# Two attentions of a two-block kernel: the first one's outputs scaled by ScalarE with remainders made a tile later, and the forgetting attention's outputs kept with two heads on the partitions

## The chip, the cores and the metric

One core of a Trainium2 chip runs the whole program once. The metric is the device time of that execution in microseconds. Engines are named as the profile names them: PE (TensorE), PEld (its weight loads), DVE (VectorE), ACT (ScalarE), POOL (GpSimd), SP (the engine whose queue issues DMAs).

## What is computed

Two transformer blocks over 1024 tokens of width 1024. The first has a convolution, a differential attention and a mixture of experts; the second mixes four branches, one of them a forgetting attention. The change concerns the two causal attentions:

```
def diff_attention(q, k, v, lam, ...):            # 4 heads, each with 2 score sets of 64, values of 128
    s = einsum("bqhcd,bkhcd->bhcqk", qi, k) * scale
    p = softmax(where(mask, s, -inf))
    a = p[:, :, 0] - lam * p[:, :, 1]
    o = einsum("bhqk,bkhe->bqhe", a, v)           # then rms_norm over each head's 128

def _fox(z, b_f):                                 # 4 heads of 64
    c = cumsum(log_sigmoid(f_pre + b_f), axis=1)
    s = einsum('bqhd,bkhd->bhqk', qi, k) + cqi[..., :, None] - c_keys[:, :, None, :]
    s = where(kpos <= qpos, s, -inf)
    out = einsum('bhqk,bkhd->bqhd', softmax(s), v)
```

## The kernel before

Both attentions are one function, `soft_attention`, called with the tag `da` (paired: `outs` = 1 output per pair, `dv` = 128, four pairs, one for each head) and with the tag `fx` (not paired: two heads per pair, `outs` = 2, `dv` = 64, two pairs). It works through units `u` = (pair `i`, query tile `t` of 128 queries), eight tiles a pair, each against `t + 1` key tiles, for two score sets `x` = 0, 1. Queries and keys are kept as a rounded part (made by ACT, L838, L841 and for fx L843) and a remainder (made by DVE, L880 for keys, L885 for queries, each 64x1024), so that scores are sums over both. Those of the next pair are made during this one: ACT rounds at the end of the units t = 1 to 4 and DVE makes the remainders at the end of the same units.

Each engine has its own queue, written out by hand and run in order:

- PE, per unit u: `scores(u + 1, 1)` (L789 to L791; waits for exps of unit u, x = 1, since the bank is the same), `scores(u + 2, 0)` (waits for exps of u + 1, x = 0), `turn_weights(u)` (L804: transposes of the exps, in chunks of up to four tiles that go alternately to two banks; a chunk waits until the one two before it was copied out), `weigh(u - 1)` (L816: the turned weights times the values; waits for the finish of unit u - 3, whose bank it takes).
- DVE, per unit u: `combine(u)` (L906 reciprocal of the row sums into `share`; in da also L909 and L911, which join both exps), `finish(u - 2)` (L918: the output bank times `share`, into `o`; waits for weigh), `peaks(u + 1, 1)` and `peaks(u + 2, 0)` (L901: row maxima of the scores), `keep_turned(u)` (L895: in fx alone, copies of the turned exps of x = 1), then the remainders.
- ACT, per unit u: `exps(u + 1, 0)`, `exps(u + 1, 1)` (L850; each waits for its peaks and reads out the row sum), `keep_turned(u)` (L860: copies of turned exps, of x = 0), then the rounding.

In da the output of a unit has queries on the partitions, 128 columns; it is normalised by the stage `on`. In fx a unit's output also has queries on the partitions, 64 columns for each of two heads, in columns 256 to 511 of `o_soft`; the window attention puts its own into columns 0 to 255. After the window attention and the mLSTM, the stage `tm` (`turn`: L1706 copies a token tile on DVE, L1716 transposes it in pieces of 128, L1726 copies out on ACT) turns all 512 columns into `yT[:, 4:8]`. The mLSTM's output goes to `o_mlstm`. The turned weights of fx lie in `yT[:, 4:8]` while the attention runs. PSUM has eight banks: 0 to 3 scores, 4 and 5 turned chunks, 6 and 7 outputs of alternate units.

Elsewhere, in `rwkv_chunks` (earlier in the second block), L2796 is a matmul whose stationary operand is 64 columns wide and whose output lies on the partitions 0 to 63 and 64 to 127 in turn, with 128 columns:

```
def sum_own(t):
    for j in range(2):
        for n, left in enumerate((vt, uw[:, :, 0:N])):
            for e in range(2):
                last = mm(pair(5, P)[side(e), j], left[:, 2 * j + e, :], n12[:, 1 - n, 2 * j + e, :],
                          start=(n == 0), stop=(n == 1))
```

## Time and profile before

| | |
|---|---|
| median of 3 runs | 3487.06 us (3474.16 to 3507.37) |
| the profiled execution | 3475.44 us, span 3473.8 us |
| PE busy | 2908.6 us (84%) |
| DVE busy | 1807.6 us (52%) |
| ACT busy | 1340.1 us (39%) |
| mean granted clock of TensorE | 0.90 of full |
| da (first attention) | 376 to about 532 us |
| fx (forgetting attention) | 2262 to about 2372 us |
| tm (turning of `o_soft`) | 2546 to about 2555 us |

Busy times are for the whole span; the stages follow each other with a barrier of all engines between them, so an engine's share of the whole says nothing about one stage. The clock column of a window is the granted clock of TensorE as a share of its full 2.4 GHz; 0.5 is its lower level, 1.2 GHz. One matmul of fp32 operands is two instructions, each with its weight load.

### The profile page before, as it was taken

The numbers are of one execution on the slowest core, as the hardware profiler recorded it, in microseconds if no ns is written. First come the engines' busy times: TensorE is split into PE (matmuls) and PEld (weight loads), VectorE is DVE, ScalarE is ACT, GpSimd is POOL, SyncE is SP. The second block draws the span as 40 slices with busy tenths as digits, with TensorE's granted clock in tenths as the row PEclk, the third lists the DMA queues.
The fourth block names the chain that finished last, engine by engine and source line by source line (L and its number), as shares of the span: only waits on it lengthen the run. The fifth ranks groups of instructions, "written<-read, shape, count | busy, mean of one in ns | idle before, by whom it ended". The sixth has DMA issues, their size and how long they took to land. (4 is left out here: it accounts for less than half of the span.)

```text
span 3473.8 us, 42813 instructions
## 1 busy us (share of the span) xinstructions
PE 2908.6 (84%) x14243; PEld 2349.4 (68%) x14243; DVE 1807.6 (52%) x2199; ACT 1340.1 (39%) x1942; POOL 287.0 (8%) x215
## 2 busy tenths in 40 slices
PE   3996587998938999997399979278777899999998
PEld 2784575665736888886377778166656688887876
DVE  2896773111437999996435255654434433333334
ACT  3222562111316888885323124254434322222232
POOL 0221000000011111111122110000200000000000
PEclk8998788999968999998599989578769799999999
DMA  2115102110249999996412220201203111111122
GB/s 80 37 49 186 44 1 79 42 48 12 85 129 332 412 412 412 412 412 265 158 43 73 65 70 2 108 2 25 49 21 130 49 48 48 48 48 33 48 100 79
DMA packets 247386, 408.19 MB, mean 118 GB/s; under 512 B 39453, under 2 KB 157268, under 8 KB 247284
## 3 DMA queue, kind: packets, MB, share of 16 engines
q1 hardware_dynamic: 215428, 343.54, 27.7%
q10 hardware_dynamic: 22464, 33.32, 2.7%
q0 software_dynamic: 9392, 29.99, 2.6%
q8 instruction: 62, 1.02, 0.1%
q14 instruction: 40, 0.33, 0.0%
HBM read 342.72 MB, written 64.07 MB: 117 GB/s over the span
## 5 line engine op out<-in xcount | busy, mean ns | idle before, releaser
L1610 DVE TENSOR_TENSOR e_w_lo<-e_ring,e_w_hi 128x1024 fp32r<-128x1024 f32 x384 | 446.5, 1217 | 48.7 <-ACT e_w_hi L1537 48.7
L1537 ACT CAST e_w_hi<-e_ring 128x1024 fp32r<-128x1024 f32 x384 | 377.6, 1049 | 38.0 <-PE banks L1467 27.4
L1939 PE MATMUL banks<-h_hi,u_w_hi 128*128 128x512 f32 x704 | 274.8, 390 | 10.5 <-DVE u_w_lo L1973 10.5
L1940 PE MATMUL banks<-h_lo,u_w_hi 128*128 128x512 f32 x704 | 274.7, 390 | 0.0
L1941 PE MATMUL banks<-h_hi,u_w_lo 128*128 128x512 f32 x704 | 274.5, 390 | 0.0
L1465 PE MATMUL banks<-e_w_hi,e_xT_hi 128*128 128x512 f32 x512 | 203.1, 397 | 0.0
L1467 PE MATMUL banks<-e_w_hi,e_xT_lo 128*128 128x512 f32 x512 | 200.1, 391 | 0.0
L1466 PE MATMUL banks<-e_w_lo,e_xT_hi 128*128 128x512 f32 x512 | 199.9, 390 | 0.0
L522 DVE SCALAR_TENSOR_TENSOR conv<-x_first,vectors,conv 128x1024 f32<-128x1024 f32 x120 | 183.8, 1531 | 9.0
L1939 PEld LDWEIGHTS banks<-h_hi,u_w_hi 128*128 128x128 f32 x704 | 132.6, 188 | 38.4 <-issue 10.9
L1941 PEld LDWEIGHTS banks<-h_hi,u_w_lo 128*128 128x128 f32 x704 | 132.6, 188 | 27.8
L1940 PEld LDWEIGHTS banks<-h_lo,u_w_hi 128*128 128x128 f32 x704 | 132.6, 188 | 27.4
L1793 PE MATMUL banks<-fd_w_hi,fd_s_hi 128*128 128x512 f32 x352 | 138.4, 393 | 10.2 <-DVE fd_s_lo L1852 9.0
L381 PE MATMUL banks<-h_hi,z_w_hi 128*128 128x512 f32 x320 | 129.1, 403 | 16.6 <-POOL z_w_lo L473 16.6
L1795 PE MATMUL banks<-fd_w_hi,fd_s_lo 128*128 128x512 f32 x352 | 137.5, 391 | 0.0
L1794 PE MATMUL banks<-fd_w_lo,fd_s_hi 128*128 128x512 f32 x352 | 137.5, 391 | 0.0
L330 PE MATMUL banks<-consts,n_xn 128*128 128x128 f32 x192 | 44.7, 414 | 98.7 <-ACT n_xn L279 98.6
L383 PE MATMUL banks<-h_hi,z_w_lo 128*128 128x512 f32 x320 | 127.2, 398 | 0.0
L382 PE MATMUL banks<-h_lo,z_w_hi 128*128 128x512 f32 x320 | 127.2, 397 | 0.0
L1978 DVE TENSOR_SCALAR yT<-yT,vectors 128x1024 f32<-128x1024 f32 x22 | 17.9, 814 | 194.2 <-ACT yT L1953 194.2
L1948 ACT ACTIVATE u_w_hi<-yT 128x1024 fp32r<-128x1024 f32 x44 | 46.5, 1057 | 178.9 <-PE banks L1941 172.7
L1973 DVE TENSOR_TENSOR u_w_lo<-yT,u_w_hi 128x1024 fp32r<-128x1024 f32 x44 | 53.8, 1222 | 115.2 <-ACT u_w_hi L1948 115.2
(528 smaller groups left out, 6689.8 us busy)
## 6 DMA issues: line engine op xcount, KB each, us to landing
e_ring<-in_w_gate_e_dram SPq DMA_DIRECT2D x128, 512.0 KB, 8.0
e_ring<-in_w_up_e_dram SPq DMA_DIRECT2D x128, 512.0 KB, 9.6
e_ring<-in_w_down_e_dram SPq DMA_DIRECT2D x128, 512.0 KB, 7.2
yT<-in_ffn_w_up_dram SPq DMA_DIRECT2D x44, 512.0 KB, 3.9
expert_results<-nothing SPq DMA_DIRECT2D x1, 16384.0 KB, 55.5
expert_results<-e_y ACTq DMA_DIRECT2D x32, 512.0 KB, 7.8
fd_w<-in_ffn_w_down_dram SPq DMA_DIRECT2D x44, 256.0 KB, 2.6
z_w<-in_w_in_dram SPq DMA_DIRECT2D x19, 512.0 KB, 3.9
```

The costliest lines, as they stand in the source:

```text
L522: nc.vector.scalar_tensor_tensor(conv[:, c, :], y[:, c, j:j + S], tap(j), conv[:, c, :], ALU.mult, ALU.add)
L1465: mm(bank, xT_hi[:, b, k, :], w_hi[:, part, cols], start=(k == 0), stop=False)
L1466: mm(bank, xT_hi[:, b, k, :], w_lo[:, part, cols], start=False, stop=False)
L1467: last = mm(bank, xT_lo[:, b, k, :], w_hi[:, part, cols], start=False, stop=(k == KT - 1))
L1537: nc.scalar.copy(w_hi[:, part, :], experts.ring[:, slot, :]).then_inc(w_rounded, 1)
L1610: tt(w_lo[:, part, :], experts.ring[:, slot, :], w_hi[:, part, :].bitcast(F32), ALU.subtract).then_inc(w_split, 1)
L1793: nc.tensor.matmul(K.ps[:, t, :], s_hi[:, b, tokens], w_hi[:, b, :], start=first, stop=False)
L1794: nc.tensor.matmul(K.ps[:, t, :], s_hi[:, b, tokens], w_lo[:, b, :], start=False, stop=False)
L1795: mm = nc.tensor.matmul(K.ps[:, t, :], s_lo[:, b, tokens], w_hi[:, b, :], start=False, stop=last)
L1939: nc.tensor.matmul(bank, w_hi[:, up, k, :], h_hi[:, k, tokens], start=(k == 0), stop=False)
L1940: nc.tensor.matmul(bank, w_hi[:, up, k, :], h_lo[:, k, tokens], start=False, stop=False)
L1941: mm = nc.tensor.matmul(bank, w_lo[:, up, k, :], h_hi[:, k, tokens], start=False, stop=(k == KT - 1))
```

## The change

Three edits. In da, DVE's `finish` is replaced by one on ACT (a copy with a per-partition scale), placed between `exps(u + 1, 0)` and `exps(u + 1, 1)`, for unit u - 2. In both attentions DVE makes the remainders one unit later (t = 2 to 5); ACT rounds where it did. In fx `weigh` exchanges its operands: a head's 64 value columns are stationary, the turned weights move, and the two heads' outputs lie on the partitions 0 to 63 and 64 to 127 with queries along the columns. Two more matmuls per unit spread `share` over the same layout, into the other columns of the same bank; DVE copies that, drains, and multiplies, straight into `yT[:, 6:8]`. So `o_soft` has half its columns, `tm` turns half as much, and the turned weights of odd units lie in `o_mlstm`. A new semaphore `shared` tells that `share` is there.

```diff
--- before.py
+++ after.py
@@ -705,7 +705,8 @@
-def soft_attention(K, tag, q_tiles, k_tiles, values, v_col, dv, o, o_col, paired, exps_room, turned_room, decay=None):
+def soft_attention(K, tag, q_tiles, k_tiles, values, v_col, dv, o, paired, exps_room, turned_room, decay=None):
@@ -724,6 +725,7 @@
     kept = [K.sem(f"{tag}_kept{x}") for x in range(outs)]
     k_made, q_made, k_split, q_split, filled, scored, peaked, exped, combined, turned, weighed, finished = (K.sem(f"{tag}_{n}") for n in
         ("k_made", "q_made", "k_split", "q_split", "filled", "scored", "peaked", "exped", "combined", "turned", "weighed", "finished"))
+    shared = K.sem(f"{tag}_shared")
     decay_landed = [K.sem(f"{tag}_decay_landed{i}") for i in range(pairs)] if decay is not None else None
     with ExitStack() as scope, nc.Block() as block:
         q1 = K.sb(scope, f"{tag}_q1", [P, 4, S], F32R)
@@ -745,7 +747,10 @@
             return K.ps[:, 2 * x:2 * x + 2, :].rearrange("p b n -> p (b n)")[:, 0:n]
         def out_bank(u):
-            return K.ps[:, 6 + u % 2, 0:outs * dv]
+            return K.ps[:, 6 + u % 2, 0:P]
+        def share_bank(u):
+            return K.ps[:, 6 + u % 2, P:2 * P]
         def exps_of(u, x):
             return exps_room[u % 2][x][:, 0:units[u][1] + 1, :]
@@ -811,10 +816,18 @@
                     pe.wait_ge(finished, u - 1)
                 for x in range(outs):
                     pe.wait_ge(kept[x], last_chunk[u, x][1])
-                    col = v_col + (i if paired else 2 * i + x) * dv
+                if paired:
                     for j in range(t + 1):
-                        last = mm(out_bank(u)[:, x * dv:(x + 1) * dv], turned_room[u % 2][x][:, j, :], values[:, j, col:col + dv],
+                        last = mm(out_bank(u), turned_room[u % 2][0][:, j, :], values[:, j, v_col + i * dv:v_col + (i + 1) * dv],
                                   start=(j == 0), stop=(j == t))
+                else:
+                    pe.wait_ge(shared, u + 1)
+                    for j in range(t + 1):
+                        for x in range(2):
+                            col = v_col + (2 * i + x) * dv
+                            mm(out_bank(u)[own(x)], values[:, j, col:col + dv], turned_room[u % 2][x][:, j, :], start=(j == 0), stop=(j == t))
+                    for x in range(2):
+                        last = mm(share_bank(u)[own(x)], share[:, x, t:t + 1].to_broadcast([P, HD]), K.const("ident"), start=True, stop=True)
                 last.then_inc(weighed, 1)
             for u, x in ((0, 0), (0, 1), (1, 0)):
@@ -860,6 +873,12 @@
                     nc.scalar.activation(turned_room[u % 2][x][:, j0:j0 + count, :],
                                          K.ps[:, 4 + c % 2, 0:count * P].rearrange("p (j n) -> p j n", n=P), ACT.Copy).then_inc(kept[x], 1)
+            def finish(u):
+                i, t = units[u]
+                act.wait_ge(shared, u + 1)
+                act.wait_ge(weighed, u + 1)
+                nc.scalar.activation(o[:, t, i * dv:(i + 1) * dv], out_bank(u), ACT.Copy, scale=share[:, 0, t:t + 1]).then_inc(finished, 1)
             for x in range(2):
                 round_keys(0, x)
                 round_queries(0, x)
@@ -869,9 +888,14 @@
                 if u + 1 < len(units):
                     for x in range(2):
                         exps(u + 1, x)
+                        if paired and u >= 2 and not x:
+                            finish(u - 2)
                 keep_turned(u)
                 if 1 <= t <= 4 and i + 1 < pairs:
                     (round_keys if t % 2 else round_queries)(i + 1, (t - 1) // 2)
+            if paired:
+                for u in (len(units) - 3, len(units) - 2, len(units) - 1):
+                    finish(u)
         @block.vector
         def _(dve):
@@ -903,7 +927,7 @@
             def combine(u):
                 i, t = units[u]
                 dve.wait_ge(exped, 2 * u + 2)
-                nc.vector.reciprocal(share[:, :, t], mass[:, :, t])
+                nc.vector.reciprocal(share[:, :, t], mass[:, :, t]).then_inc(shared, 1)
                 dve.drain()
                 if paired:
                     nc.vector.tensor_scalar(factor[:, t:t + 1], mass[:, 0, t:t + 1], share[:, 1, t:t + 1], K.lam[:], ALU.mult, ALU.mult)
@@ -914,9 +938,10 @@
             def finish(u):
                 i, t = units[u]
                 dve.wait_ge(weighed, u + 1)
-                place = o[:, t, o_col + i * outs * dv:o_col + (i + 1) * outs * dv]
-                nc.vector.tensor_tensor(place.rearrange("p (x n) -> p x n", x=outs), out_bank(u).rearrange("p (x n) -> p x n", x=outs),
-                                        share[:, 0:outs, t].unsqueeze(2).to_broadcast([P, outs, dv]), ALU.mult).then_inc(finished, 1)
+                place = o[:, i, t * P:(t + 1) * P]
+                nc.vector.tensor_copy(place, share_bank(u))
+                dve.drain()
+                nc.vector.tensor_tensor(place, out_bank(u), place, ALU.mult).then_inc(finished, 1)
             def fill(dst, value):
                 ones = K.const("ones")[0:HD, 0:1].to_broadcast([HD, S])
@@ -935,17 +960,18 @@
                 peaks(u, x)
             for u, (i, t) in enumerate(units):
                 combine(u)
-                if u >= 2:
+                if not paired and u >= 2:
                     finish(u - 2)
                 if u + 1 < len(units):
                     peaks(u + 1, 1)
                 if u + 2 < len(units):
                     peaks(u + 2, 0)
                 keep_turned(u)
-                if 1 <= t <= 4 and i + 1 < pairs:
-                    (split_keys if t % 2 else split_queries)(i + 1, (t - 1) // 2)
-            for u in (len(units) - 2, len(units) - 1):
-                finish(u)
+                if 2 <= t <= 5 and i + 1 < pairs:
+                    (split_queries if t % 2 else split_keys)(i + 1, (t - 2) // 2)
+            if not paired:
+                for u in (len(units) - 2, len(units) - 1):
+                    finish(u)
             dve.drain()
@@ -2988,7 +3014,7 @@
             with ExitStack() as exps_scope:
                 exps = K.sb(exps_scope, "da_exps", [P, 2, NT, P])
                 room = lambda n: qkv[:, :, HALF + n * P:HALF + (n + 1) * P]
-                soft_attention(K, "da", qkT[:, 0:HEADS], qkT[:, HEADS:2 * HEADS], qkv, 2 * HALF, VD, o, 0, True,
+                soft_attention(K, "da", qkT[:, 0:HEADS], qkT[:, HEADS:2 * HEADS], qkv, 2 * HALF, VD, o, True,
                                [[exps[:, b], room(2 + b)] for b in range(2)], [[room(b)] for b in range(2)])
             conv = K.sb(right, "conv_again", [P, CT, S], side="right")
             oT = K.sb(right, "oT", [P, HEADS, S], side="right")
@@ -3059,7 +3085,7 @@
         K.window_bias, K.sinks = (K.sb(scope, name, shape, side="right")
                                   for name, shape in (("window_bias", [P, 4, 2 * P]), ("sinks", [P, 4])))
         K.mlstm_keys = K.sb(scope, "mlstm_keys", [P, 4 * NT], side="right")
-        o = K.sb(scope, "o_soft", [P, NT, 2 * RW], side="right")
+        o = K.sb(scope, "o_soft", [P, NT, RW], side="right")
         o_mlstm = K.sb(scope, "o_mlstm", [P, NT, RW], side="right")
         Z["values"], Z["mlstm_o"] = sb("values", [P, NT, 3 * RW]), sb("mlstm_o_kept", [P, 2, S])
         values = Z["values"]
@@ -3074,11 +3100,12 @@
                              (Z["total"][:, 0, :], mlstm["rise"][:, 0], mlstm["rise"][:, 1])])
             tiles_of = lambda ap: ap.rearrange("p (j n) -> p j n", n=P)
             exps = [[tiles_of(gates[:, 0, :]), tiles_of(gates[:, 1, :])], [tiles_of(gates[:, 2, :]), tiles_of(Z["mlstm"][:, 0, 0:S])]]
-            turned = [[tiles_of(yT[:, 4 + 2 * b + n, :]) for n in range(2)] for b in range(2)]
-            soft_attention(K, "fx", Z["fox_q"][:], Z["fox_k"], values, RW, HD, o, RW, False, exps, turned, decay=decay)
+            flat = o_mlstm[:].rearrange("p t n -> p (t n)")
+            turned = [[tiles_of(yT[:, 4 + n, :]) for n in range(2)], [tiles_of(flat[:, n * S:(n + 1) * S]) for n in range(2)]]
+            soft_attention(K, "fx", Z["fox_q"][:], Z["fox_k"], values, RW, HD, yT[:, 6:8, :], False, exps, turned, decay=decay)
         window_attention(K, "sw", R["swa_q"], R["swa_k"], values, 2 * RW, o, 0)
         mlstm_attention(K, "ml", mlstm, values, 0, o_mlstm, 0)
-        turn(K, "tm", o, yT[:, 4:8, :])
+        turn(K, "tm", o, yT[:, 4:6, :])
         group_norm_and_turn(K, "mn", o_mlstm[:], 4, K.vec("mlstm_norm_2", 0, 2), yT[:, 2:4, :], gate=Z["mlstm_o"][:])
     K.recycle()
     return yT
```

## Rows read from the trace of the kernel before

**Rows 1.** Windows of da and fx: us, busy (x instructions) by engine, clock, DMA, GB/s
```profile
376.00:533.00 157.00, 116.39 (x688) 102.10 (x688) 114.95 (x213) 96.65 (x203) 0.00 (x0) 0.86 0.00 1
2262.00:2374.00 112.00, 86.43 (x560) 80.31 (x560) 58.73 (x105) 53.23 (x105) 2.11 (x4) 0.80 0.01 1
```

**Rows 2.** Waits: who <- for whom: us in total, times, longest; da, then fx
```profile
ACT qkv L850 <- DVE da_low L901: 50.9, 32, 3.0
...
DVE da_q L885 <- ACT da_q L841: 9.0, 6, 1.8
...
DVE da_k L880 <- ACT da_k L838: 8.5, 6, 1.7
...
DVE fx_k L880 <- ACT fx_k L838: 1.2, 2, 0.6
```

**Rows 3.** Timeline of da, third pair: start, us, engine, line, op [idle <-releaser]
```profile
468.72 2.13 ACT L838 ACTIVATE da_k<-x_first 64x1024 fp32r<-64x1024 f32 x2
...
469.80 1.22 DVE L880 TENSOR_TENSOR da_k<-x_first,da_k 64x1024 fp32r<-64x1024 f32 x1 [1.24 <-ACT da_k L838]
470.87 0.69 ACT L850 ACTIVATE da_exps<-banks,da_low 128x512 f32<-128x512 f32 x1
...
471.70 0.79 PE L789 MATMUL banks<-da_k,da_q 128*128 128x512 f32 x1 [2.30 <-ACT da_exps L850]
...
472.97 0.69 ACT L850 ACTIVATE qkv<-banks,da_low 128x512 f32<-128x512 f32 x1 [1.32 <-DVE da_low L901]
...
474.15 0.49 ACT L860 ACTIVATE qkv<-banks 128x384 f32<-128x384 f32 x1 [0.40 <-PE banks L804]
...
479.17 0.79 ACT L850 ACTIVATE qkv<-banks,da_low 128x640 f32<-128x640 f32 x1 [2.82 <-DVE da_low L901]
...
492.34 1.01 ACT L850 ACTIVATE qkv<-banks,da_low 128x896 f32<-128x896 f32 x1 [3.01 <-DVE da_low L901]
...
493.47 0.17 DVE L906 RECIPROCAL da_share<-da_mass 128x2 f32<-128x2 f32 x1
```

**Rows 4.** The finishing line L918: forms with ns minimum/median/maximum
```profile
L918 DVE TENSOR_TENSOR qkv<-banks,da_share x32: 281/283/293, 395.8 to 531.4; 128x128 f32<-128x128 f32 x32
```

**Rows 5.** Timeline of fx, one tile of the second pair (t = 5)
```profile
2343.40 0.48 PE L789 MATMUL banks<-fx_k,fx_q 128*128 128x512 f32 x1
...
2343.63 0.29 DVE L918 TENSOR_TENSOR o_soft<-banks,fx_share 128x128 f32<-128x128 f32 x1 [0.88 <-PE banks L816]
...
2344.56 2.26 DVE L901 TENSOR_REDUCE fx_low<-banks 128x1 f32<-128x896 f32 x2 [0.64 <-PE banks L791]
...
2345.68 1.01 ACT L850 ACTIVATE z_gates<-banks,fx_low 128x896 f32<-128x896 f32 x1 [3.56 <-DVE fx_low L901]
...
2347.41 0.84 PE L804 MATMUL banks<-consts,z_mlstm 128*128 128x128 f32 x6 [1.20 <-ACT yT L860]
...
2348.10 2.34 PE L816 MATMUL banks<-values,yT 128*128 128x64 f32 x20
...
2350.25 0.48 PE L789 MATMUL banks<-fx_k,fx_q 128*128 128x512 f32 x1
```

**Rows 6.** Timeline of fx, the weighing of the next tile, at the lower clock
```profile
2355.48 5.22 PE L816 MATMUL banks<-values,yT 128*128 128x64 f32 x24
```

**Rows 7.** Timeline of PE where L2796 stands between forms of other shape
```profile
2153.99 0.58 PE L2814 MATMUL banks<-rs_q,rs_diagonal 128*128 128x32 f32 x4
2154.51 0.44 PE L2796 MATMUL banks<-rs_n,rs_vt 128*64 128x128 f32 x4
2154.78 0.39 PE L2796 MATMUL banks<-rs_n,rs_uw 128*64 128x128 f32 x4
...
2155.21 0.39 PE L2796 MATMUL banks<-rs_n,rs_uw 128*64 128x128 f32 x4
2155.53 0.44 PE L2743 MATMUL banks<-consts,z_rwkv 128*128 128x128 f32 x2
```

**Rows 8.** Groups by line in tm: count, busy us, mean ns, idle before
```profile
L1716 PE MATMUL banks<-consts,tm_stage 128*128 128x128 f32 x32 | 6.9, 383 | 2.8 <-DVE tm_stage L1706 2.2 <-issue 0.4
```

## The prediction

> **What bounds the kernel now.** The page comes first: it shows a program of many stages one after the other, each between barriers, so an edit is worth what it changes in its own stage. The busy shares of whole engines say nothing here. The stretches come next [rows 1]. The first attention (tag da) lasts 157 us with PE, DVE and ACT each busy 97 to 116 us; the forgetting attention (tag fx) lasts 112 us with PE busy 86 and DVE and ACT under 60. So da is bound by a ring of three engines, fx mostly by PE and what stands in series with it. The third stage touched, tm (the turning of `o`), lasts about 9 us. Together they are 278 us, 8% of the 3473.8 us span, so 1% of the kernel (35 us) would be an eighth of them.
>
> Then the waits of these stretches [rows 2]. In da ACT waits 50.9 us in 32 times for DVE's peaks (L901), always before the second exps; DVE itself waits 9.0 and 8.5 us at L885 and L880, the remainders, for ACT's rounded copies (6 times each: three changes of head pair, four splits each). In fx that wait is 1.2 us.
>
> Last the timelines. In da [rows 3] the tile t=1 of the last but one pair: ACT rounds keys from 468.72, DVE stands 1.24 us before L880 and splits until 471.02, and only then comes combine, although the second exps it needs were done before ACT took up the rounding at 468.72. The second exps of the next tile so start at 472.97 after 1.32 us of waiting, the one after at 479.17 after 2.82. In fx [rows 5] one tile's turn of the ring is 6.85 us (2343.40 to 2350.25), everything in series: scores on PE, peaks from 2344.56, exps from 2345.68, ACT's turned copy, PE's second turning from 2347.41, and then weigh(u-1), 20 instructions from 2348.10 to 2350.25, ahead of the next scores. The turned chunks share two banks, so the second head's turning waits for ACT's copy, which stands behind exps(u+1, 1). Weigh is thus paid in full there.
>
> **da, finish moved to ACT.** DVE loses 32 L918 of 0.283 us [rows 4], of which about 0.21 from start to next start is paid where DVE is full. ACT gains one scaled copy of 128x128 per tile; that operation is not in the stage. Bounds: nothing, to the 0.79 us of a 128x640 exps [rows 3]; nearest in kind is its own DVE form, so 0.3 us. It lies between exps(u+1, 0) and exps(u+1, 1), where ACT waits 1.6 us on average [rows 2], so it is hidden; if that cover were gone, 28 x 0.3 = 8 us. Queued behind its wait for weigh(u-2) is exps(u+1, 1), for which combine waits; weigh(u-2) ends before the scores those exps need, as both stand in PE's order, so it adds nothing.
>
> **da, remainders a tile later.** I follow the two queues through the change of pair of rows 3, every instruction with the length it has there before. Tile 2: combine(2) starts at 468.7 instead of 471.0, and exps(3, 1) come right after exps(3, 0) at 471.7 instead of 472.97. But the turned copy of tile 2 stays at 474.15: PE takes scores(4, 0) first, at 471.70, which wait for exps(3, 0) of 470.87, and those stand behind ACT's rounding. So of the first wait nothing is kept. Tile 3: the keys' remainder, its input long there, fills DVE from 474.3 to 475.5, combine(3) ends at 476.7, peaks(4, 1) at 477.4, and exps(4, 1) start there instead of at 479.17: 1.7 us. The turned copy, which now waits for PE, comes 1.6 earlier and with it ACT's next rounding. Tile 4: the same again, exps(5, 0) 1.6 and exps(5, 1), after the finish on ACT, 3.1 us earlier, the turned copy, again bound by PE, 2.4. Tile 5: combine(5) and peaks(6, 1) back to back end at 488.2, where exps(6, 1) start instead of at 492.34: 4.1. Then the fourth remainder, which now stands in a tile where DVE is full, costs 1.2 back: combine(6) starts at 490.6 instead of 493.47, and peaks(7, 1), with finish gone, come 3.1 earlier. From tile 7 to tile 1 of the next pair PE is the bound and passes the 3.1 on. Three changes: 9.3 us. The last pair has no remainders to make and gains five times 0.21: 1.0. Together 10.3. The ends: nothing (ACT and PE set the pace everywhere as in tile 2), and all 17.5 us of waits plus 28 x 0.21 = 23 us; I take the middle because the hand-followed queues show both kinds of tile.
>
> **fx, weigh with two heads on the partitions.** Stationary is now a head's 64 columns of values, moving the 128 columns of turned weights; 288 instructions (2 passes x 72 key tiles x 2 heads) stay 288, since only the roles of the operands change. Before: 20 in 2.34 us and, next to it, 2.15 from start to start, 0.11 each; at the lower clock level 24 in 5.22, 0.21 each [rows 5, 6]. The same form already stands in the kernel, L2796 (128*64, output 128x128, sides alternating): two groups of four take from 2154.78 to 2155.21, 0.054 an instruction [rows 7]; at half the clock I take twice that. About 68 of the 288 ran at the lower level (both groups of 24 and the first small ones), so 220 x 0.057 + 68 x 0.10 = 19.4 us. Added are the shares: two matmuls per unit, 64 instructions, at 0.054 with a quarter slower: 4.2 us. A stationary operand repeated from one column is not in the rows; from below it costs nothing, from above the 0.11 of a full one, 7 us; I take the middle form's.
>
> The change of array shape twice a unit: L2814 to L2796 0.52 us for four, first L2796 group 0.27 instead of 0.215, L2796 to L2743 0.32 instead of 0.215 [rows 7]: about 0.2 us a unit, 3.2 us over 16. If every switch waited for a matmul to run out (a group of four takes 0.39, less three spacings of 0.054: 0.23), 32 of them would be 7.4 us, 4.2 more. The Trainium skill, TensorEngine Tiling (Array Packing), section Tiling Modes, says that changing the mode, unlike changing the tile, drains TensorE; the row shows a switch but less than such a full run-out, and the sum goes by the row. Net 19.4 - 4.2 - 3.2 = 12.0; at t=1 to 3 of the first pair ACT's rounding is the bound and hides part: 11.5 kept.
>
> **fx, finish on DVE** becomes copy, drain, multiply: 0.28 + 0.08 + 0.29 against 0.29 [rows 4], 0.37 more. In the large tiles it is covered: L918 starts at 2343.63, peaks only at 2344.56 [rows 5]. In about 7 small tiles peaks follow at once, and at the very end it is bare: +2.9 us. Uncovered everywhere: 16 x 0.37 = 6. The wait for `shared` is long met when weigh comes.
>
> **fx, remainders.** One change of pair; waits of 1.2 [rows 2]. The split at t=1 leaves a tight tile and that at t=5 falls into DVE's wait for weigh: -2 us (0 to -4).
>
> **tm** turns two tiles of 128 instead of four: 16 of 32 L1716 go, 0.2 us each from start to start at the lower clock (PE busy 6.9 us for 32 [rows 8]): 3.4 less, of which 3.0 in the ring with DVE's and ACT's copies (1 to 4). The smaller `o` and the new place of the turned weights move no work.
>
> **Sum**: -10.3 - 11.5 + 2.9 - 2.0 - 3.0 = -23.9 us. The profiled execution took 3475.4 (its span and 1.6 around it): 3451.5. It lies 11.6 under the median 3487.06 of three runs that spread over 33 us; against the median the forecast is 3463.
>
> **Rivals.** (1) Little is kept: in da the ACT-PE chain of the first step holds at all four splits, and in fx the next wait takes half of weigh's gain. For it: exps(3, 0) behind rounding; against it: ACT waits 50.9 us for DVE. -1 - 5.8 + 2.9 - 1 - 2 = -7: 3480. (2) All waits and the whole of weigh are kept: -23 - 12 - 4 - 4 + 0.4 = -43: 3444. For it: the series ring of rows 5; against it: splits still cost their 1.2 us. (3) Slower: TensorE's clock. In fx it was granted 0.80 on average [rows 1], and the group of 24 after PE's idle time ran at the 1.2 GHz level [rows 6]. Weigh is the dense part; halved, PE is idle for a larger share. New PE work is about 86 - 12 = 74 us at 0.80; the gain is eaten when it stretches by a third, at a mean clock of 0.61; at 0.50 it stretches by 0.6, +44: 3507. Against it: the ring gets shorter in time too, and its idle parts (peaks, exps) don't grow. The Trainium skill, TensorE: Matmul & The Clock Gate, section "A second HAM failure mode", says that frequent small idle times between groups of matmuls make the clock swing between its levels; the fx rows agree in kind. (4) Full run-out at each switch: 3467.
>
> **Chances.** Forecast 0.56, (1) 0.20, (2) 0.12, (3) 0.06, (4) 0.06. The forecast's own range is 3452 to 3473. Reaching into (1) and (2), and leaving their far ends and (3) out, 3441 to 3485. 1% is about what a measurement of this kernel can tell from no change; 3452 is the bound: below it lie (2) and an edge of the forecast, 0.17; slower by 1% (3522) needs (3) in da too: 0.03; between them 0.80.
>
> **What would show it.** In the profile after: weigh at 0.054 an instruction, and fx about 100 us; L880 and L885 of da with no wait for ACT, da about 147 us; ACT's scaled copy 0.3 us, with no wait for PE before it; tm about 6 us. It is wrong if the new finish on ACT waits for PE, if fx's granted clock is under 0.7, or if other stages differ by more than these.

## The result and the profile after

Eight runs of the changed kernel had a median of 3465.06 us (3462.80 to 3473.57), eight of the kernel before 3492.11 (3474.16 to 3507.37). The ratio is 0.9926, with a 95% interval of 0.9904 to 0.9949: 27 us of medians against the 24 forecast, less than 1%. The profiled execution took 3470.72 us, only 4.7 under that of before and 19 over the 3451.5 that the prediction gave for it, a gap to be explained below.

The stretches first (us, then busy time and instructions of PE, its weight loads, DVE, ACT and POOL, granted clock, DMA share, GB/s), as in [rows 1]. da is 7.5 us shorter by these windows, fx 13 us; DVE has given 6.7 us away in da and ACT has taken 9.5; in fx PE has given 14.5 us away, and its clock has risen from 0.80 to 0.86.

```profile
372.50:522.00 149.50, 111.13 (x688) 98.61 (x688) 108.23 (x182) 106.14 (x235) 0.00 (x0) 0.89 0.00 1
2272.00:2371.00 99.00, 71.98 (x624) 60.51 (x624) 61.94 (x121) 52.74 (x105) 2.11 (x4) 0.86 0.01 1
```

The windows have some slack at their edges. Below a stage is measured from the start of its first reciprocal (L906 before, L930 after) to the end of its last finish (L918; after, L880 in da and L944 in fx):

```profile
L930 DVE RECIPROCAL da_share<-da_mass x32: 150/167/169, 383.8 to 513.5; 128x2 f32<-128x2 f32 x32
...
L880 ACT ACTIVATE qkv<-banks,da_share x32: 351/368/388, 391.8 to 520.0; 128x128 f32<-128x128 f32 x32
...
L930 DVE RECIPROCAL fx_share<-fx_mass x16: 153/158/169, 2285.4 to 2360.3; 128x2 f32<-128x2 f32 x16
...
L944 DVE TENSOR_TENSOR yT<-banks,yT x16: 290/292/293, 2291.4 to 2369.2; 128x128 f32<-128x128 f32 x16
```

So da is 520.4 - 383.8 = 136.6 us (144.4 before, whose first reciprocal stood at 387.3 and whose last finish [rows 4] at 531.4) and fx 84.1 us (96.7 before). tm went from 8.8 to 6.0 us; 16 turnings are left, as against [rows 8] (ns minimum/median/maximum, first and last start):

```profile
L1742 PE MATMUL banks<-consts,tm_stage x16: 418/421/474, 2546.2 to 2550.9; 128*128 128x128 f32 x16
```

Together -7.8 - 12.6 - 2.8 = -23.2 us, against -23.9 forecast. The windows give 149.5 us for da and 99.0 for fx, where the prediction had about 147 and 100.

**da, the waits** after (engine line waited for: us, times, longest), to be set beside [rows 2]:

```profile
ACT qkv L863 <- DVE da_low L925: 24.3, 26, 2.4
...
DVE da_low L925 <- PE banks L796: 22.8, 22, 2.8
...
ACT qkv L873 <- PE banks L809: 9.9, 8, 1.8
...
ACT qkv L880 <- PE banks L821: 5.7, 8, 1.4
...
DVE da_share L930 <- ACT qkv L863: 5.1, 7, 1.3
```

ACT's wait for the peaks has gone from 50.9 to 24.3 us, and the two rows of DVE waiting for ACT's rounded copies are gone. In their place DVE waits for the scores and ACT for the turnings, both from PE: the bound has moved to PE with ACT. The new finish (L880) waits for PE in 8 of 32 tiles, which the forecast had excluded.

**da, the change of pair of [rows 3]** in the timeline after (start, us, engine, line, operation, idle before it):

```profile
465.77 1.21 DVE L904 TENSOR_TENSOR da_k<-x_first,da_k 64x1024 fp32r<-64x1024 f32 x1
...
469.02 0.80 ACT L863 ACTIVATE qkv<-banks,da_low 128x640 f32<-128x640 f32 x1 [0.87 <-DVE da_low L925]
...
469.99 1.22 DVE L909 TENSOR_TENSOR da_q<-x_first,da_q 64x1024 fp32r<-64x1024 f32 x1
...
472.57 0.90 ACT L863 ACTIVATE da_exps<-banks,da_low 128x768 f32<-128x768 f32 x1
...
473.47 0.36 ACT L880 ACTIVATE qkv<-banks,da_share 128x128 f32<-128x128 f32 x1
473.72 0.90 ACT L863 ACTIVATE qkv<-banks,da_low 128x768 f32<-128x768 f32 x1
...
480.22 1.01 ACT L863 ACTIVATE qkv<-banks,da_low 128x896 f32<-128x896 f32 x1 [0.96 <-DVE da_low L925]
...
481.60 1.22 DVE L909 TENSOR_TENSOR da_q<-x_first,da_q 64x1024 fp32r<-64x1024 f32 x1
...
482.85 0.17 DVE L930 RECIPROCAL da_share<-da_mass 128x2 f32<-128x2 f32 x1
```

The splits (L904, L909) start with no wait, and the fourth (481.60) stands bare in front of the reciprocal of tile 6. At the start of this stretch the kernel after is already 8.15 us ahead (reciprocal of tile 1: 457.41 against 465.56). With that taken off, the steps followed come out like this, in us earlier than before:

| | forecast | measured |
|---|---|---|
| turned copy, tile 2 | 0 | 0.3 |
| exps(4, 1) | 1.7 | 2.0 |
| exps(5, 1) | 3.1 | 3.6 |
| turned copy, tile 4 | 2.4 | 2.2 |
| exps(6, 1) | 4.1 | 4.0 |
| combine(6) | 2.9 | 2.5 |
| exps(7, 1) | 3.1 | 2.65 |

**fx, the tile of [rows 5] and the one behind it**, after:

```profile
2347.53 0.50 PE L794 MATMUL banks<-fx_k,fx_q 128*128 128x512 f32 x1
...
2348.01 0.29 DVE L944 TENSOR_TENSOR yT<-banks,yT 128x128 f32<-128x128 f32 x1
...
2348.71 2.27 DVE L925 TENSOR_REDUCE fx_low<-banks 128x1 f32<-128x896 f32 x2 [0.41 <-PE banks L796]
...
2351.57 0.85 PE L809 MATMUL banks<-consts,z_mlstm 128*128 128x128 f32 x6 [1.19 <-ACT o_mlstm L873]
...
2352.34 1.31 PE L828 MATMUL banks<-yT,values 128*64 128x128 f32 x20
...
2353.48 0.39 PE L830 MATMUL banks<-consts,fx_share 128*64 128x128 f32 x4
...
2353.80 0.50 PE L794 MATMUL banks<-fx_k,fx_q 128*128 128x512 f32 x1
...
2359.75 2.48 PE L828 MATMUL banks<-o_mlstm,values 128*64 128x128 f32 x24
```

The turn of the ring is 2353.80 - 2347.53 = 6.27 us (6.85 before). The 20 of the weighing take 1.14 us to the first share instead of 2.15. The group of 24 behind it still runs at the lower clock level, 0.10 us an instruction, but for 2.48 us where it had 5.22 [rows 6]. DVE's multiply (2348.01) is over 0.41 us before the peaks can start.

**Where the profiled spans differ.** The spans, 3473.8 and 3469.0 us, are 4.8 apart, the three stages 23.2. Most of the rest was found in a stretch that the change doesn't touch, called the routing here: from the last matmul that reads `m_w_hi` to the last that reads `e_w_hi`, which is the output projection, the routing and the experts. It lasts 784.9 us before and 800.4 after, 15.5 more. The products with the router's weights, before (L1149) and after (L1175), PE of each kernel (count, busy us, mean ns, idle):

```profile
L1149 PE MATMUL banks<-r_w,r_h2T 128*128 128x36 f32 x128 | 14.9, 275 | 0.0
```

```profile
L1175 PE MATMUL banks<-r_w,r_h2T 128*128 128x36 f32 x128 | 27.7, 400 | 0.0
```

And the windows over that loop, of before and of after (granted clock third from the end):

```profile
973.10:993.20 20.10, 19.60 (x177) 19.26 (x176) 12.96 (x13) 7.17 (x7) 0.00 (x0) 1.00 0.41 166
```

```profile
959.70:996.30 36.60, 36.60 (x177) 36.60 (x176) 13.18 (x13) 7.17 (x7) 0.00 (x0) 0.50 0.22 90
```

The same 177 instructions take 20.1 us at 2.4 GHz or 36.6 at 1.2 GHz: 16.5 us, against 18.4 missing. What is left is spread over other untouched stages, which by themselves move by some us from profile to profile (the stage ml lasted 83.5 to 91.5 us in the fourteen profiles, from its first output copy to its last).

### The profile page after: what moved, and what is told of

Read it like the earlier page. It is cut to its first block and busy times, and to the rows that moved or that the text cites. A ratio compares the mean times of both kernels' runs of the same rounds, so it can differ in the third digit from the quotient of the medians.

```text
span 3469.0 us, 42989 instructions
## 1 busy us (share of the span) xinstructions
PE 2904.5 (84%) x14291; PEld 2346.2 (68%) x14291; DVE 1802.1 (52%) x2183; ACT 1347.3 (39%) x1974; POOL 289.4 (8%) x215
## 5 line engine op out<-in xcount | busy, mean ns | idle before, releaser
L1965 PE MATMUL banks<-h_hi,u_w_hi 128*128 128x512 f32 x704 | 274.8, 390 | 10.6 <-DVE u_w_lo L1999 10.6
```

The costliest lines, as they stand in the source:

```text
L1965: nc.tensor.matmul(bank, w_hi[:, up, k, :], h_hi[:, k, tokens], start=(k == 0), stop=False)
```

## The experiments

Stage lengths of the profiled execution of each kernel, in us; "routing" is the stretch defined above, "r_w" the mean of one product with the router's weights. A median of one run is that profiled run.

| kernel | da | fx | two groups of 24 in fx | routing | r_w, ns | median us (runs) |
|---|---|---|---|---|---|---|
| before | 144.4 | 96.7 | 5.00, 5.22 | 784.9 | 275 | 3492.11 (8) |
| before_again | 144.5 | 97.7 | 5.22, 5.22 | 784.6 | 275 | 3476.69 (1) |
| after | 136.6 | 84.1 | 2.81, 2.48 | 800.4 | 400 | 3465.06 (8) |
| after_again | 134.8 | 84.1 | 2.79, 2.46 | 797.7 | 400 | 3466.33 (1) |
| da_undone | 144.7 | 84.1 | 2.82, 2.49 | 794.9 | 346 | 3472.79 (10) |
| fx_undone | 134.8 | 93.6 | 5.22, 2.79 | 797.4 | 399 | 3484.06 (10) |
| finish_undone | 140.4 | 81.4 | 1.53, 2.68 | 799.3 | 400 | 3480.32 (1) |
| shift_undone | 140.8 | 84.7 | 2.83, 2.75 | 798.6 | 400 | 3473.00 (1) |
| heads_apart | 137.0 | 90.7 | not whole | 800.6 | 400 | 3478.87 (1) |
| shares_thrice | 134.8 | 86.2 | 1.53, 2.37 | 798.0 | 400 | 3471.98 (1) |
| finish_late | 137.1 | 83.8 | 2.57, 2.83 | 798.6 | 399 | 3472.22 (1) |
| keep_first | 134.9 | 80.5 | 1.53, 1.53 | 799.8 | 399 | 3464.29 (5) |
| router_warm | 134.9 | 83.7 | 2.32, 2.63 | 783.6 | 275 | 3451.05 (4) |
| keep_first_warm | 134.8 | 78.7 | 1.53, 1.53 | 783.2 | 279 | 3450.34 (4) |

In the old form a group of 24 lasts 2.79 us at the upper level and some 5.2 at the lower, in the new form 1.53 and 2.8; lengths between them belong to groups in which the level changed.

### Both kernels again

No edit. 

> The kernel before, a second profile. The first two profiles differ by 4.8 us of span while the medians differ by 27, because the routing stage between the first block's matmuls and the experts took about 15 us longer in the profile of after. My theory: that stage varies from run to run by itself, so its length in this profile lies anywhere within some 15 us of the first, while da (first reciprocal of combine to the last finish) is again 144.4 us, fx 96.8 us and tm 8.8 us, each within 0.5. Rival: the routing stage is longer because of the change (another placement in memory); then it is 219.5 us again here, to 1 us, and 234 in the second profile of after.

> The changed kernel, a second profile. Theory: da 136.5 us, fx 84.0, tm 5.5, each within 0.5; the routing stage's length is not bound to the kernel. Rival (the change lengthens routing): 234 us again.

The second pair of profiles gives da -9.7 and fx -13.6. A stage repeats to 1 or 2 us, not to the 0.5 expected; da of the changed kernel came out at 134.8 and at 136.6 without any edit. The lower clock in the routing was there again in after (400 ns) and not in before (275). So my theory, that this stretch varies by itself whatever the kernel, got no support here: its length went with the kernel, as the rival had it.

### da_undone: the first attention as before, the rest as after

```
-                if 2 <= t <= 5 and i + 1 < pairs:
+                if 2 <= t <= 5 and i + 1 < pairs and not paired:
...
+                if 1 <= t <= 4 and i + 1 < pairs and paired:
+                    (split_keys if t % 2 else split_queries)(i + 1, (t - 1) // 2)
```

and the finish of da by DVE, as in finish_undone. 

> The changed kernel with da as before: finish on DVE and remainders at t = 1 to 4 in da; fx and tm changed. Theory (gains of the stages add, nothing is handed on across barriers): da 144.4 us, fx 84.0, tm 5.5; 19.5 us of the gain stays, of 3465 against the kernel before 16 to 20 us less. Rival (the layout of memory or the clock carries something from one stage to another): fx differs by more than 2 us from 84.0.

Measured: da 144.7, fx 84.1; ratio to before 0.9948 (0.9922 to 0.9974), with 3489.03 (19 runs) before. By medians that is 16.2 us less, as expected. So da's 8 to 10 us and fx's 12.6 are independent of each other, and each stays in its stage.

Its routing shows that the clock level can change within the loop. Entered at 972.69 us, the loop took 1.87 us for each of its first three groups of 16 products, the upper level. Then PE stood idle for 0.92 us, the next group took 2.79, and from there on a group took 3.47, the lower level.

### fx_undone: the forgetting attention's outputs as before, its remainders a tile later

The loops of weigh, finish, `o_soft` with 2 * RW columns and the turning of four tiles are those of before. 

> The changed kernel with fx in its old form (queries on the partitions, one multiply as finish, o_soft with 512 columns turned); its remainders stay a tile later. Theory: da 136.5 us, fx 94.8 (96.8 less 2.0 by the later remainders), tm 8.8; against the kernel before 9 to 11 us less. Rival: the later remainders do nothing in fx, fx 96.8. A third: they bring 4, fx 93.

Measured: fx 93.6 against 84.1 and tm back at four tiles; ratio 0.9996 (0.9976 to 1.0016), not the 9 to 11 us less that were expected. fx is 3.1 us under before, with nothing but the later remainders in it. The table says what that is: its second group of 24 ran at the upper level, 2.79 us where before had 5.22. Of the 3.1 us 2.4 are the clock of one group, and only 0.7 is left for the split itself. By its stages this kernel should lie 9.6 (da) + 3.1 = 12.7 us under before if both had the routing loop at the same level, and level with it if all runs of before had that loop at the upper one (12.5 for the routing). The interval, 8 us under to 6 us over, excludes the first. So, as far as these stage lengths carry, before had the loop at the upper level in more of its runs than fx_undone.

### finish_undone and shift_undone: the two edits of da one by one

```
+                if paired:
+                    nc.vector.tensor_tensor(o[:, t, i * dv:(i + 1) * dv], out_bank(u),
+                        share[:, 0, t:t + 1].to_broadcast([P, dv]), ALU.mult).then_inc(finished, 1)
+                    return
...
-                        if paired and u >= 2 and not x:
-                            finish(u - 2)
```

> The changed kernel with da's finish back on DVE between combine and peaks; remainders a tile later in both. da was 144.4 us before and 134.4 to 136.5 in the changed kernel. My sum gives the finish about 0.21 us in five tiles of each of four pairs, 4 us, and the later remainders the rest: da 139 to 140 here. Rival (the finish does most): 142 or more. Rival (the finish is worth nothing, PE and ACT hide it): 135 to 136.

```
-                if 2 <= t <= 5 and i + 1 < pairs:
-                    (split_queries if t % 2 else split_keys)(i + 1, (t - 2) // 2)
+                if 1 <= t <= 4 and i + 1 < pairs:
+                    (split_keys if t % 2 else split_queries)(i + 1, (t - 1) // 2)
```

> The changed kernel with the remainders at t = 1 to 4 again in both attentions; finish on ACT. Theory: da 144.4 less 4 for the finish, 140 to 141, with DVE's wait for ACT's rounded copies back at 17 us; fx 84.0 plus 2 to 3.5. Rival (the shift does little in da): 137 or less.

With both undone da is 144.7, with finish alone undone 140.4, with the shift alone undone 140.8, with neither 134.8 or 136.6. Each edit brings 4 us by itself and 4 to 6 on top of the other, and together they are all of da's gain. In fx, where shift_undone has the remainders at their old place, the stage is 84.7 instead of 84.1 us, and 0.3 of these 0.6 are a longer group of 24; 2 to 3.5 were expected. ACT's wait for DVE, finish undone:

```profile
ACT qkv L863 <- DVE da_low L920: 37.4, 29, 2.6
```

and shift undone, where DVE's waits for ACT's rounded copies are back as in [rows 2]:

```profile
ACT qkv L863 <- DVE da_low L925: 35.8, 32, 2.6
...
DVE da_q L909 <- ACT da_q L854: 9.1, 6, 1.8
...
DVE da_k L904 <- ACT da_k L851: 8.5, 6, 1.7
```

Of 50.9 us of waits the shift alone takes 13.5 and the finish alone 15.1, and some 4 of each reach the end of the stage.

### finish_late: ACT's finish behind the second exps

```
-                        if paired and u >= 2 and not x:
+                        if paired and u >= 2 and x:
```

> The changed kernel with ACT's finish of da after exps(u + 1, 1) instead of before, where nothing covers it: exps(u + 1, 1) end what combine and the next scores wait for, and ACT's turned copy stands behind the finish. Theory: the copy comes 0.25 to 0.37 us later in tiles where ACT is not ahead of PE, da 134.4 to 136.5 grows by 2 to 6 us. Rival (ACT has slack there too): da unchanged within 1 us.

da 137.1 us. With its code unedited da took 134.8 to 137.0 (heads_apart), so the 2 to 6 us expected didn't come. So neither is it shown that the place between the exps is the better one, nor that the 5.7 us for which L880 waits there cost anything.

### heads_apart: the weighing of one head after the other

```
-                    for j in range(t + 1):
-                        for x in range(2):
+                    for x in range(2):
+                        for j in range(t + 1):
```

> The changed kernel, but fx weighs one head after the other (all key tiles of partitions 0 to 63, then all of 64 to 127) instead of in turn. What makes an instruction 0.054 us: the narrower stationary operand (64 columns to load instead of 128), or that neighbouring matmuls lie on different columns of the array and overlap? Theory (narrow load): still 0.054 an instruction, fx 84 us. Rival (alternation): 0.08 to 0.11 an instruction within a head, 288 of them, fx 92 to 100 us.

The same 288 instructions, only in another order: fx 90.7 us, 6.6 over after, half of what the change brought to the stage, and nearer to the rival's 92 to 100 than to the theory's 84. PE of heads_apart, timeline of one weighing:

```profile
2315.22 1.69 PE L828 MATMUL banks<-yT,values 128*64 128x128 f32 x17
2316.65 0.32 PE L830 MATMUL banks<-consts,fx_share 128*64 128x128 f32 x1
2316.75 0.27 PE L828 MATMUL banks<-yT,values 128*64 128x128 f32 x1
2316.81 0.27 PE L830 MATMUL banks<-consts,fx_share 128*64 128x128 f32 x1
2316.86 0.38 PE L828 MATMUL banks<-yT,values 128*64 128x128 f32 x2
```

17 instructions take 1.53 us to the next of their kind, 0.090 each; 25 and 29 take 2.40 and 2.84 (0.096 to 0.098). In the old form it was 0.11, alternating it is 0.057. My account of the gain, a weight load of half the columns, can explain at most what the exchange brings without alternation, about a quarter to two fifths. The rest comes from alternation: successive instructions use different halves of the array's columns. The likely reading is that work in one half doesn't wait for work in the other, and the rows above fit it: in PE's program the share products (L830) come behind all 20 instructions of L828, yet the first of them, for the other half, is recorded ahead of the last three, and where the halves mix, the starts are 0.05 to 0.10 us apart. Which part of an instruction overlaps, the load or the run, isn't shown.

### shares_thrice: the two share products of each unit made three times

```
-                    for x in range(2):
+                    for x in (0, 1, 0, 1, 0, 1):
                         last = mm(share_bank(u)[own(x)], ...
```

It adds 4 matmuls to each unit, 128 instructions in all. 

> The changed kernel, each unit of fx with its two share matmuls issued three times (the same values written again): 128 instructions more. Theory (weigh and the shares are in series with the rest of the ring): 0.054 us each in full, at the lower clock 0.11, so 7 to 9 us more: fx 91 to 93. Rival (PE has slack there, another engine sets the pace): under 3 us more, fx under 87.

```profile
2353.96 2.37 PE L828 MATMUL banks<-o_mlstm,values 128*64 128x128 f32 x24
2356.17 0.82 PE L830 MATMUL banks<-consts,fx_share 128*64 128x128 f32 x12
```

Twelve share instructions last 0.82 us where four last 0.39: 0.054 each, so a stationary operand repeated from one column costs what any other of 64 columns does. 128 of them are 6.9 us. fx rose by 2.1 to 86.2, but its first group of 24 ran 1.3 us faster than in after; against finish_undone, which has the fx of after and whose first group ran at that level too, it is 4.8. So, with the clock allowed for, half to 70% of the added work stood in series. That allowance is argued: the bare 2.1 us lies under the 3 us that I had named for the rival, slack on PE, and far under the 7 to 9 expected.

### keep_first: in fx, ACT's turned copy ahead of its second exps

```
+                        if not paired and not x:
+                            keep_turned(u)
-                keep_turned(u)
+                if paired or u + 1 == len(units):
+                    keep_turned(u)
```

In the tile of fx shown above, PE waits for this copy ahead of its second turning (1.19 us at 2351.57). 

> The changed kernel, but in fx ACT copies out the turned exps of its head (keep_turned) between exps(u + 1, 0) and exps(u + 1, 1) instead of after both, so that PE's second turning and weigh no longer stand behind peaks and exps of the next unit. Theory (that order closes the series ring of fx): at t = 5 a tile goes from 6.05 us to what PE itself has to do, about 5, at t = 6 from 7.4 to 5.5, less at others; fx 84.0 to 73 to 76 us, and the whole 8 to 11 us under the changed kernel. Rival: exps(u + 1, 1) now come later, since the copy waits for PE's turning, and the ring only changes its order: fx within 2 us of 84. The clock: PE's idle gaps shrink, and no weighing runs at the lower level.

```profile
2345.50 0.50 PE L794 MATMUL banks<-fx_k,fx_q 128*128 128x512 f32 x1
...
2348.90 0.85 PE L809 MATMUL banks<-consts,z_mlstm 128*128 128x128 f32 x6 [0.56 <-ACT o_mlstm L873]
...
2351.14 0.50 PE L794 MATMUL banks<-fx_k,fx_q 128*128 128x512 f32 x1
...
2354.50 1.53 PE L828 MATMUL banks<-o_mlstm,values 128*64 128x128 f32 x24
```

That is PE's timeline in keep_first. The tile's turn is 5.64 us instead of 6.27, PE waits for the copy for half as long, and both groups of 24 run at the upper level, which is 2.2 of the 3.6 us that fx loses (84.1 to 80.5). ACT now waits for PE instead:

```profile
ACT o_mlstm L873 <- PE banks L809: 17.7, 8, 3.2
...
ACT yT L873 <- PE banks L809: 15.5, 8, 3.0
```

The gain was less than half of the expected one. The new waits suggest why: at its new place the copy is bound by the turning. In the whole time it can't be seen (3464.29, ratio 0.9929, 0.9908 to 0.9951).

### router_warm and keep_first_warm: matmuls in PE's idle time ahead of the routing

```
+            for _ in range(30):
+                nc.tensor.matmul(K.ps[:, 7, 0:P], K.const("ident"), K.const("ident"), start=True, stop=True)
             pe.wait_ge(landed, 80)
```

30 products of the identity with itself (60 instructions), in a bank that the stage doesn't use yet; they only add work. 

> The changed kernel with 30 matmuls of the identity into an unused bank while PE waits for its first rows in the routing stage (norm_and_route, which the change doesn't touch). There PE's 128 router matmuls took 275 ns each in both profiles of the kernel before and 400 ns in both of the changed one, the granted clock being 0.75 to 0.83 and 0.50, and the stage took 13 to 16 us longer. Theory (TensorE comes into the loop at its lower level after an idle stretch, and stays there, as a matter of timing): the loop runs at 275 ns here, the first matmuls to the experts' start 13 us shorter in the profile, and the time 5 to 13 us less than the changed kernel's. Rival (memory or placement sets it): 400 ns again.

> Both edits, the earlier copy in fx and the 30 matmuls before the routing. Theory (they are in different stages and add): fx 73 to 76 us, router matmuls at 275 ns, 15 to 22 us less than the changed kernel, 40 to 50 us less than the kernel before. Rival: one of them moves the other's clock and the gains don't add.

PE's timeline in router_warm, and behind it the group of the products:

```profile
948.10 8.72 PE L1162 MATMUL banks<-consts 128*128 128x128 f32 x60 [9.87 <-PEq L1779]
956.65 1.06 PE L1169 MATMUL banks<-consts,r_h 128*128 128x128 f32 x8
```

```profile
L1177 PE MATMUL banks<-r_w,r_h2T 128*128 128x36 f32 x128 | 14.9, 275 | 0.0
```

The 60 instructions lie in an idle time that after has too (17.99 us before the first turning at 956.03). The first turnings now take 1.06 us for 8 instead of 3.92 for 16, the products are back at 275 ns, the routing at 783.6 us. router_warm has a median of 3451.05 (ratio 0.9901, 0.9871 to 0.9930), keep_first_warm 3450.34 (0.9894, 0.9869 to 0.9919), each 14 us under the same kernel without the added matmuls (3465.06, from other runs, and 3464.29); for router_warm 5 to 13 were expected. keep_first_warm was expected 15 to 22 us under after, with fx at 73 to 76 us; it came 14.7 under, with fx at 78.7. Both lie more than 35 us under the 3487.46 (8 runs) of before on that chip.

## Why the prediction was right

**What bounds the kernel.** The runs agree with it: a ring of three engines in da, where either edit alone brings 4 us, and PE with what stands in series in fx; no gain or loss went from one of these two stages to the other (da_undone and fx_undone).

**da.** Forecast -10.3, measured -7.8 and -9.7. The steps followed came to within 0.5 us in the one change of pair that can be laid beside them. But the term built on them was put too high: from the reciprocal of tile 1 to that of the next pair's tile 1, the three changes of pair took 37.7, 38.3 and 38.3 us before and 35.6, 35.8 and 35.6 after (35.1, 35.6 and 34.5 in after_again). So a change gave 2.2 to 2.6 us (2.6 to 3.7), where 3.1 was taken three times, and the last pair 0.65 instead of 1.0. Neither edit was the main one: 4 us each. ACT's scaled copy was put at 0.3 us and lasted 0.368. That it adds no wait for PE was wrong, it waits in 8 tiles, 5.7 us together; the exps behind it wait for DVE anyway (0.87 and 0.96 us in the rows above), so there it is covered. It was one of the signs that should have shown the forecast wrong, and was set too sharply. Another of these signs came true as well, and heavily: other stages differ, the routing by 15.5 us.

**fx, weigh.** The size held: 0.057 an instruction against 0.054 to 0.057. All groups of weigh sum to 40.1 us before and 21.6 after, 18.5 less, against 19.4 forecast. The reason behind it did not hold as a plain price of the form, since the rows that it was taken from [rows 7] alternate their sides. heads_apart shows that without the alternation the same form costs 0.09 to 0.098, and half of the stage's gain is gone. The kernel does alternate, so the number was that of the right row; that alternation was what mattered in it was not seen.

**The shares and the switches.** Forecast 4.2 and 3.2 us. 0.054 for each share (shares_thrice) is 3.5 for 64. For the switches: six instructions of the turning are 0.66 us, and the weighing starts 0.77 behind their start; four shares are 0.215, and the scores start 0.32 behind. That is 0.1 a switch and 0.2 a unit, as taken. The full run-out of rival (4), 0.23 a switch, fell. The Trainium skill, TensorEngine Tiling (Array Packing), section Tiling Modes, speaks of a drain at each change of mode; in these rows it comes to 0.1 us.

**fx as a whole**, -10.6 forecast, -12.6 and -13.6 measured. The sum is near, the terms less so. Weigh saved 0.051 us an instruction at the upper level (all its groups there would sum to 33.9 us before and 19.2 after, an estimate from the groups that ran so), where 0.057 was taken; the clock gave part of that back, since by the groups' lengths about 60 instructions ran at the lower level before and 48 after, where 68 were counted for both. The term that the prediction lacks is the clock of fx's other matmuls, which the change doesn't touch. It took them as they were. The scores and the turnings were busy 73.4 us before and 70.3 after, 3.1 less, most of it in the turnings (75.8 and 70.4 in the second pair of profiles). Against rival (3) the clock rose when weigh got shorter, from 0.80 to 0.86. Kernels with the same code of fx show how much hangs on it: 81.4 us with one group of 24 at the lower level, 83.7 to 84.1 with both there for all or most of their length; the group itself is 1.3 of the difference. The remainders (-2.0) were put too high: fx_undone's 3.1 us are 2.4 of clock and 0.7 of split, and undoing them alone (shift_undone) cost 0.6.

**finish on DVE** was to cost 2.9 us. It was not measured by itself. In the tile shown it is covered, as forecast. The terms that were measured (18.5 - 3.5 - 3.2 + 3.1 + 0.6) come to about 15.5 us, and the stage gained 12.6; that leaves 3 us for this finish and for what the small tiles hide of weigh, forecast 2.9 and 0.5. It is an estimate, as busy time is not all in series.

**tm.** Forecast -3.0, measured -2.8.

**The sum.** -23.2 us in the first pair of profiles, -25 in the second, -27 by the medians, -23.9 forecast. Rivals (1) with -7 and (2) with -43 both fell by the stages' lengths. What the prediction did not see is the routing: it made the profiled span only 4.8 us shorter, and in the second pair 10.4. That the medians still moved by 27 us, as the three stages did, is explained only if most of those runs of before had the loop at the lower level too. That is argued, not shown, as only the profiles tell the level in the loop, and in both of before it was the upper one. Three things speak for a before that has it at either level. Its runs spread over 33 us where after's spread over 11. Its profiled executions (3475.4, 3476.7) lay well under its medians (3487 to 3492). And of the 19 runs of before that da_undone is compared with, the nine shortest (3476.1 to 3486.1 us) have a mean granted clock of 0.899 to 0.901, the ten longest (3489.0 to 3511.7) 0.892 to 0.898. Then the eight runs of before in the result, seven of them at 3487 or more, would compare like with like. In so far as the forecast of the whole came true by the state of a loop that it never looked at, it was lucky; the stages' lengths were not.

A rival stays open: that the change itself puts the loop at the lower level, by an earlier entry or otherwise, and so gives away part of its gain. In all nine profiles with one of da's edits or both, and no matmuls added, the loop was entered at 959 to 968 us and ran at the lower level throughout (399 or 400 ns). In the three with da as before it was entered at 973 to 975 us at the upper level, and kept it in two. The matmuls of router_warm bring it to the upper level either way.

## What to carry to other kernels

Compare two profiles stage by stage: 16 us of clock in an untouched loop had nearly hidden 23 us of gain in the spans. Where a stage is a ring of engines, follow two or three of its turns by hand with the durations of the trace; it gave each step of one change of pair here within 0.5 us, though not the stage's sum (forecast 10.3, measured 7.8 and 9.7). Put narrow matmuls in pairs that alternate the halves of the array's columns (0.057 against 0.090 to 0.098 us here). And look what TensorE did ahead of a dense loop: here 8.7 us of added matmuls fitted into its idle time there and brought 14 us.

## What the runs showed of the hardware

- A stationary operand of 64 columns with 128 columns moving, fp32: 0.057 us an instruction when successive ones alternate the column halves, 0.090 to 0.098 when they stay in one, 0.11 for 128 columns with 64 moving. Changing between the 64-column and the 128-column form costs 0.1 us.
- TensorE stayed at 1.2 GHz (granted clock 0.50) through a loop of 36.6 us in which it is recorded busy all the time, after 18 us of idle time. The same loop after the same idle time was at 2.4 GHz in both profiles of before. 8.7 us of matmuls in that idle time brought the upper level in both kernels that had them, and 14 us of whole time. In da_undone the level fell inside the loop, after 0.92 us of idle time. What tips it without the added matmuls stays open: no run varied the moment of entry alone. The Trainium skill, TensorE: Matmul & The Clock Gate, section "Why this matters for your kernels", advises warming TensorE up with matmuls ahead of a measurement; here it is worth it inside the kernel.
- A scaled copy by ScalarE of 128x128 from PSUM lasts 0.368 us, the same multiply by VectorE 0.283 [rows 4].
- The clock level of a burst is not settled by the code nor by the idle time right before it: identical code in fx ran a group of 24 in 1.53, 2.3 or 2.8 us, in kernels that differed only hundreds of us earlier. The idle time ahead of the turning before it was 2.27 us in both of these (after, then finish_undone):

```profile
2320.30 1.30 PE L809 MATMUL banks<-consts,z_gates 128*128 128x128 f32 x7 [2.27 <-ACT yT L873]
2321.53 2.81 PE L828 MATMUL banks<-o_mlstm,values 128*64 128x128 f32 x24
```

```profile
2329.12 0.95 PE L809 MATMUL banks<-consts,z_gates 128*128 128x128 f32 x7 [2.27 <-ACT yT L873]
2330.00 1.53 PE L828 MATMUL banks<-o_mlstm,values 128*64 128x128 f32 x24
```
